# A fifth merged pair of weight rows in the second column half of w_out

## The chip, the cores and the metric

The kernel runs on one core of a Trainium2 chip. The metric is the device time of one execution in microseconds (us). Engines: TensorE (PE; PEld is its weight load), VectorE (DVE), ScalarE (ACT), GpSimd (POOL) and SyncE (SP), which here issues nearly all DMAs.

## The reference

One decoder layer on 256 tokens of width 2048, all in float32:

```
h = rms_norm(x);  proj = h @ w_in
o_sb = stick_breaking_attention(8 heads);  o_ds = indexed_sparse_attention(8 heads)
merged = sigmoid(g_sb) * (o_sb @ w_branch[:1024]) + sigmoid(g_ds) * (o_ds @ w_branch[1024:])
x = x + merged @ w_out                      # 2048 x 2048
h = rms_norm(x);  u = causal_depthwise_conv(h @ w_up)
x = x + (silu(gate) * val) @ w_down
```

The change is about `merged @ w_out`.

## The kernel before, in words

**Three matmuls for a product.** Every float32 operand is split into a high part and the rest (low). ACT makes the high part `hi` of a weight chunk, DVE subtracts it to make `lo`, and TensorE adds up three matmuls: left-high by right-high, left-low by right-high, left-high by right-low. One such group of three, 128 rows by 512 columns, is called a product here.

**Chunks and slots.** Weights come in chunks numbered through the program. There are four slots of `hi` and `lo` (`SLOTS`): chunk c uses slot c % 4, and ACT may write it once TensorE has used chunk c-4 (`w_used`). ACT and DVE run three chunks ahead (`AHEAD`): the loops over c in w_out (lines 1139 and 1825) start at C_OUT + 3 and hold, behind the split of each chunk, the other work of that stretch in a fixed order. All engines work in order.

**Plain and merged pairs.** w_out is done in two column halves (m = 0 and 1) of 1024 columns, each with eight pairs of 128-row tiles. A plain pair is two chunks of four products. A merged ("summed") pair is a Strassen-like form: four chunks, the first half as wide, with seven products together (`rows_summed`). It needs sums of weight blocks, here made far ahead by DVE in three additions (`weight_terms`), stored by a DMA in `out_sums` and loaded again like weights; and sums of the activation tiles `mT` with their high and low parts (`left_m`), made in batches (`sums_whole`, `sums_diff`, `sums_rest`, `left_hi_part`, `sums_lo`).

**Order in w_out.** `OUT_ORDER`: the first half has plain 4, merged 0 and 1, plain 5, merged 2 and 3, plain 6 and 7; the second has merged 0 and 1, plain 4, merged 2 and 3, plain 5, 6 and 7. Loads go through eight raw buffers (`OUT_SLOTS`) in the order of use, 48 loads in all; the raw buffers 0 to 3 serve the other stages too. SP issues a load when the low part of the chunk that held the buffer is done.

**Ends of the halves.** Behind the last merged pair of a half ACT copies four PSUM banks (`far_copy`), DVE adds them up in eight operations and adds them to y (`out_far`, lines 1795 to 1815). The other four banks are copied at the end of the first half (`near_copy`) and added to y (`out_near`); at the end of the second half DVE adds them straight from PSUM (line 1843). ACT takes squares of y for the norm (`square`), TensorE transposes y into `h2T`, with high and low parts by ACT and DVE, and w_up starts (`up_loads`, `up_body`).

**Where the weight sums come from.** Two of the eight sums are made in row block two of w_in (b = 1, `rows_turn` on SP, line 1631 on DVE), six in the gates stage (`spare_turn`).

Of the kernel before, what the change touches and what calls it, by code (L numbers as in the profile page):

```python
# [29 lines left out]
def hybrid_layer(nc, x, positions, attn_norm_g, w_in, q_norm_g, k_norm_g, w_branch, w_out,  # L30
# [9 lines left out]
    P = 128  # L40
# [41 lines left out]
    OUT_SUMMED = 4  # L82
    OUT_AT = [C_OUT + (2 * CPG + 2 * OUT_SUMMED) * m for m in range(3)]
# [4 lines left out]
    def block_steps(orders, chunk, raw, stored):  # L88

        table = []  # L90
        for b, order in orders.items():
            for kind, pair in order:
                made = pair if kind == "summed" else None
                table.append(Step(b, pair, made, chunk, raw, stored and made is not None))
                chunk += 2 if made is None else 4
                raw += 4 if table[-1].stored else 2
            assert chunk == BLOCK_END[b]
            assert sorted(p for _, p in order) == [*range(KT // 2)]
        return table

    def turns(*pairs):
# [5 lines left out]
                 [("summed", 0), ("summed", 1), ("plain", 4), ("summed", 2), ("summed", 3),  # L107
                  ("plain", 5), ("plain", 6), ("plain", 7)]]
# [6 lines left out]
    IN_ROWS, IN_SPARE = 2, 6  # L115
    OUT_SUMS = [(m, pair) for pair in range(OUT_SUMMED) for m in range(2)]
# [8 lines left out]
    OUT_SAVED = (C_UP - C_OUT) // SLOTS - OUT_EXTRA  # L125
    ROW_SLOT = [(q + SLOTS) % (SLOTS + 2) for q in range(ROW_RAWS)]
    ROW_SLOT += [q % OUT_SLOTS for q in range(OUT_RAWS)]
    assert OUT_RAWS % OUT_SLOTS == 0
# [18 lines left out]
    S_BATCHES = 2 * S_PAIRS // 2  # L147
# [23 lines left out]
    IN_BUFFER = (IN_ROWS + IN_GATES, IN_SPARE)  # L171
    IN_ALL = sum(IN_BUFFER)

    def spare_before(g):

        return 3 * IN_ROWS + 6 * g

    def gates_before(g):

        return 3 * IN_ROWS + 3 * g + 3 * (IN_SPARE if isinstance(g, int) and g >= IN_SPARE else g + 1)  # L180
# [47 lines left out]
    def summed(m, name):  # L228

        return len(ORDER[0]) * m + ORDER[m].index(name) + 1  # L230

# [11 lines left out]
    with ctx:  # L243
# [9 lines left out]
        def sem(name):  # L253
# [79 lines left out]
                  at("left_m", [OUT_SUMMED, 4, 2, P], 48 * KB, f32r)]  # L333
        whole_s = [at("whole_h", [2, 2, S], 74 * KB), at("whole_m", [2, 2, S], 64 * KB)]
        left_sraw = [at("left_hraw", [2, 4, P], 78 * KB), at("left_mraw", [2, 4, P], 68 * KB)]
        hsum13 = at("hsum13", [2 * GRP], 74 * KB)
# [47 lines left out]
        pre_spare = at("pre_spare", [4 * GRP], 96 * KB)  # L384
        sums = nc.dram_tensor("sums", (len(SUM_ROWS) * P, 4 * GRP), f32, kind="Internal").ap()
# [26 lines left out]
        def left_pairs(i):  # L412
            src, k, n = (hT, mT)[i // 2], 2 * (i % 2), left_count(i)
            return src[:, 2 * k:2 * (k + n), :].rearrange("p (b k) (q s) -> p b k q s", b=n, q=2)

        def left_count(i):
            return min(2, (S_PAIRS, OUT_SUMMED)[i // 2] - 2 * (i % 2))


# [168 lines left out]
        def _(sp):  # L588
# [48 lines left out]

            def rows_turn(j):
# [16 lines left out]
            def load_step(step, w, col):  # L655

                for k in range(4 if step.stored else 2):
# [9 lines left out]
                    elif stage(step) and slot < SLOTS + 2:  # L667
                        wait_alone(sp, sig_done, 8 * 4)
                    elif stage(step):
                        wait_alone(sp, left_done, S_BATCHES)  # L670
# [13 lines left out]
            def gates_turn(i):  # L684
# [4 lines left out]
                def before(j):  # L689
                    if j == 0:  # L690
                        wait_alone(sp, pre_stored[0], 16 * (IN_ROWS + i) + 1)
# [7 lines left out]
            def spare_turn(g, j):  # L699

                if j == 1 and 1 <= g <= IN_SPARE:
                    e = IN_ROWS + g - 1
# [3 lines left out]
                if j == 4 and g < IN_SPARE:  # L706
                    if g == 0:
                        wait_alone(sp, w_used, C_HEADS)
                    wait_alone(sp, pre_stored[1], 16 * g + 1)
                    out_terms(IN_ROWS + g, pre_spare, pre_landed[1])  # L710
# [14 lines left out]
            wait_alone(sp, pre_stored[1], 16 * IN_SPARE + 1)  # L725
# [34 lines left out]
            up_loads(0, {(1, 0): first_load})  # L760
# [49 lines left out]
        def _(act):  # L810
# [71 lines left out]
            def chunk_hi(c):  # L882
# [18 lines left out]
                act.activation(hi[s][:, 0:width], src[:, 0:width], ACT.Copy).then_inc(hi_done, 1)  # L901

            def left_hi_part(i):

                act.wait_ge(left4_raw, i + 1)
                at_, n = 2 * (i % 2), left_count(i)
                act.activation(left_s[i // 2][:, at_:at_ + n, :, 0, :],
                               left_sraw[i // 2][:, 0:n, :, :], ACT.Copy).then_inc(left_hi, 1)
# [74 lines left out]
            def block_out(c):  # L983

                for b, end in BLOCK_END.items():
# [14 lines left out]
                    if c == end + 2 and b == S_BLOCKS[0]:  # L1000
                        act.wait_ge(pre_stored[0], 16 * IN_ROWS + 1)
# [137 lines left out]
            for c in range(C_OUT + AHEAD, C_UP + AHEAD):  # L1139
                i = c - AHEAD - C_OUT  # L1140
                chunk_hi(c)
# [3 lines left out]
                if 20 <= c - OUT_AT[1] < 24:  # L1145
                    square(c - OUT_AT[1] - 20)
# [159 lines left out]
        def _(dve):  # L1306
# [106 lines left out]
            def chunk_lo(c):  # L1413
# [7 lines left out]
                else:  # L1421
# [5 lines left out]
                    .then_inc(lo_done, 1)  # L1427
# [34 lines left out]
            def sums_whole(i):  # L1462
# [6 lines left out]
                dve.tensor_tensor(whole_s[i // 2][:, 0:left_count(i), :, :], a[:, :, :, 0, :],  # L1469
                                  a[:, :, :, 1, :], ALU.add).then_inc(whole_done, 1)  # L1470

            def sums_diff(i):

                f, d = [x_[i // 2][:, 0:left_count(i)] for x_ in (whole_s, left_sraw)]
# [7 lines left out]
            def sums_rest(i):  # L1482

                f, d = [x_[i // 2][:, 0:left_count(i)] for x_ in (whole_s, left_sraw)]
# [7 lines left out]
            def sums_lo(i):  # L1492

                at_, n = 2 * (i % 2), left_count(i)
                left = left_s[i // 2]
                dve.wait_ge(left_hi, i + 1)
                dve.tensor_tensor(left[:, at_:at_ + n, :, 1, :], left_sraw[i // 2][:, 0:n, :, :],
                                  left[:, at_:at_ + n, :, 0, :].bitcast(f32), ALU.subtract)\
# [123 lines left out]
            for c in range(C_ROWS + AHEAD, C_HEADS + AHEAD):  # L1622
# [83 lines left out]
            def gates_body(h, spare):  # L1706
                for j in range(CPG):
# [25 lines left out]
                    if spare and j in (1, 2):  # L1733
                        for k in ((0,), (1, 2))[j - 1]:
                            weight_terms(pre_spare, pre_landed[1], 48 * h + 48, 3 * IN_ROWS + 6 * h, k)
                    if j in (5, 6, 7):
                        before = 3 * IN_ROWS + 3 * h + (3 * h + 3 if spare else 3 * IN_SPARE)
                        weight_terms(pre_gates, pre_landed[0], 48 * (IN_ROWS + h) + 48, before, j - 5)
                if not spare:
                    dve.wait_ge(pre_stored[1], 16 * IN_SPARE + 1)  # L1740
# [52 lines left out]
            def out_far(m, n):  # L1793
# [15 lines left out]
                if n == 2:  # L1809
                    dve.tensor_tensor(two[:, :], five[:, :], two[:, :], ALU.subtract)\  # L1810
# [507 lines left out]
        def _(pe):  # L2318
# [215 lines left out]
            def rows_plain(step, last):  # L2534
                for k in range(2):
# [11 lines left out]
                    i.then_inc(w_used, 1)  # L2547
# [5 lines left out]
            def rows_summed(step, end):  # L2553
                b, c, k = step.m, step.chunk, step.pair
                near, far = NEAR[b], FAR[b]
                left = left_s[stage(step)]
                s1, s2, s3, s4 = [(left[:, step.made, j, 0, :], left[:, step.made, j, 1, :])
                                  for j in range(4)]
# [244 lines left out]
```

## Time and profile before

| what | value |
|---|---|
| median of 3 runs | 1426.52 us (1426.42 to 1426.78) |
| profiled execution | 1426.08 us |
| its span | 1424.4 us |
| TensorE busy | 1418.9 us, 7583 matmuls |
| DVE busy | 1203.8 us |
| ACT busy | 902.8 us |
| DMA | 373.22 MB, mean 262 GB/s |

Busy means that an instruction of that engine was at work. Matmuls overlap and their ends are modelled, so the step from one product to the next is read from the starts. Times in the rows below are from the start of the span.

### The profile page before, as it was taken

The numbers are of one execution on the slowest core, as the hardware profiler recorded it, in microseconds if no ns is written. First come the engines' busy times: TensorE is split into PE (matmuls) and PEld (weight loads), VectorE is DVE, ScalarE is ACT, GpSimd is POOL, SyncE is SP. The second block draws the span as 40 slices with busy tenths as digits, with TensorE's granted clock in tenths as the row PEclk, the third lists the DMA queues.
The fourth block names the chain that finished last, engine by engine and source line by source line (L and its number), as shares of the span: only waits on it lengthen the run. The fifth ranks groups of instructions, "written<-read, shape, count | busy, mean of one in ns | idle before, by whom it ended". The sixth has DMA issues, their size and how long they took to land.

```text
span 1424.4 us, 23622 instructions
## 1 busy us (share of the span) xinstructions
PE 1418.9 (100%) x7583; PEld 1216.2 (85%) x7583; DVE 1203.8 (85%) x1591; ACT 902.8 (63%) x1302; POOL 329.6 (23%) x365
## 2 busy tenths in 40 slices
PE   9999999999999999999999999999999999999998
PEld 7888888888888888888888888888888888888887
DVE  6878998888878767887978888988889879898998
ACT  6546667566767766667665555555555556675775
POOL 2310000423232223560012222323223232100000
PEclk9999999999999999999999999999999999999999
DMA  8776665668999876569778888888888877698896
GB/s 256 243 249 183 208 197 185 194 183 293 312 337 329 285 232 209 186 239 336 258 237 279 275 292 289 279 281 279 290 289 276 280 221 233 232 318 315 312 339 250
DMA packets 151308, 373.22 MB, mean 262 GB/s; under 512 B 14048, under 2 KB 14336, under 8 KB 146768
## 3 DMA queue, kind: packets, MB, share of 16 engines
q1 hardware_dynamic: 150176, 369.93, 77.7%
q0 software_dynamic: 896, 2.42, 0.5%
q8 instruction: 29, 0.48, 0.1%
q14 instruction: 31, 0.25, 0.0%
q10 hardware_dynamic: 176, 0.14, 0.0%
HBM read 333.64 MB, written 38.80 MB: 261 GB/s over the span
## 4 chain that ended last, share of the span: by engine, by line
PE 99%; ACT 0%; DVE 0%; POOL 0%; issue 0%; DVEq 0%; POOLq 0%
PE bank L2320 98%; PE bank L2374 0%; PE bank L2393 0%; PE bank L2598 0%; ACT hT L837 0%; PE bank L2639 0%; DVE y L2008 0%; PE bank L2462 0%; POOL lo L2121 0%; ACT hi L820 0%; PE bank L2440 0%; DVE y L2053 0%; DVEq L243 0%; POOL ident L2101 0%; PE bank L2447 0%
## 5 line engine op out<-in xcount | busy, mean ns | idle before, releaser
L1311 DVE TENSOR_TENSOR lo<-raw,hi 128x1024 fp32r<-128x1024 f32 x338 | 436.6, 1297 | 140.4 <-ACT hi L820 138.6
L820 ACT ACTIVATE hi<-raw 128x1024 fp32r<-128x1024 f32 (+1 forms) x342 | 358.9, 1052 | 262.0 <-PE bank L2320 256.0
L2320 PE MATMUL bank<-h2T,hi 128*128 128x512 f32 x1408 | 483.3, 394 | 0.0
L2320 PE MATMUL bank<-h2T,lo 128*128 128x256 f32 x1408 | 376.8, 278 | 0.0
L2320 PEld LDWEIGHTS bank<-h2T,hi 128*128 128x128 f32 x1408 | 257.9, 188 | 53.5
L2320 PE MATMUL bank<-hT,hi 128*128 128x512 f32 (+1 forms) x784 | 272.9, 395 | 0.1
L2320 PEld LDWEIGHTS bank<-h2T,lo 128*128 128x128 f32 x1408 | 264.5, 188 | 7.8
L2320 PE MATMUL bank<-hT,lo 128*128 128x256 f32 (+1 forms) x784 | 212.6, 281 | 0.0
L1258 ACT ACTIVATE hi<-raw 128x1024 fp32r<-128x1024 f32 (+1 forms) x139 | 132.6, 974 | 64.2 <-PE bank L2320 63.2
L2320 PEld LDWEIGHTS bank<-hT,hi 128*128 128x128 f32 (+1 forms) x784 | 143.9, 187 | 29.8 <-POOL lo L2121 0.5
L1982 DVE TENSOR_TENSOR lo<-raw,hi 128x1024 fp32r<-128x1024 f32 (+1 forms) x139 | 152.2, 1124 | 16.1 <-ACT hi L1258 11.6
L2320 PE MATMUL bank<-hi,hT 128*128 128x512 f32 x520 | 161.7, 392 | 0.0
L2291 POOL TENSOR_TENSOR u<-u,rms_row 128x256 f32<-128x256 f32 x88 | 88.6, 1007 | 274.6 <-DVE u L1853 274.6
L2320 PEld LDWEIGHTS bank<-hT,lo 128*128 128x128 f32 (+1 forms) x784 | 147.0, 187 | 4.0
L2320 PE MATMUL bank<-hi,ffT 128*128 128x512 f32 x486 | 149.5, 389 | 0.0
L2320 PEld LDWEIGHTS bank<-hi,hT 128*128 128x128 f32 x520 | 96.6, 188 | 20.7 <-DVE lo L1425 0.5
L2320 PEld LDWEIGHTS bank<-hi,ffT 128*128 128x128 f32 x486 | 91.2, 188 | 18.9
L2320 PE MATMUL bank<-lo,hT 128*128 128x512 f32 x260 | 101.3, 390 | 0.0
L1863 DVE SCALAR_TENSOR_TENSOR conv<-u,params,conv 128x256 f32<-128x256 f32 x176 | 87.9, 500 | 12.3 <-DVE conv L1863 3.7
L2320 PE MATMUL bank<-lo,ffT 128*128 128x512 f32 x243 | 94.5, 389 | 0.0
L2305 POOL TENSOR_TENSOR conv<-conv,silu 128x256 f32<-128x256 f32 x44 | 60.4, 1373 | 116.3 <-DVE conv L1863 116.3
L2320 PE MATMUL bank<-oT,hi 128*128 128x512 f32 x256 | 86.9, 394 | 0.0
(293 smaller groups left out, 2021.8 us busy)
## 6 DMA issues: line engine op xcount, KB each, us to landing
raw<-in_w_up SPq DMA_DIRECT2D x176, 512.0 KB, 4.6
raw<-in_w_in SPq DMA_DIRECT2D x160, 512.0 KB, 4.6
raw<-in_w_down SPq DMA_DIRECT2D x61, 512.0 KB, 5.7
raw<-sums SPq DMA_DIRECT2D x54, 512.0 KB, 5.8
sums<-pre SPq DMA_DIRECT2D x19, 1024.0 KB, 6.3
raw<-in_w_branch SPq DMA_DIRECT2D x32, 512.0 KB, 4.2
pre<-in_w_down SPq DMA_DIRECT2D x19, 512.0 KB, 5.2
pre<-in_w_down SPq DMA_DIRECT2D x38, 256.0 KB, 5.6
```

Source lines behind the costliest of these rows:

```text
L820: act.activation(hi[s][:, 0:width], raw[s][:, 0:width], ACT.Copy)\
L1258: act.activation(hi[c % SLOTS][:, 0:width], src[:, 0:width], ACT.Copy)\
L1311: dve.tensor_tensor(lo[s][:, 0:width], raw[s][:, 0:width], hi[s][:, 0:width].bitcast(f32), ALU.subtract)\
L1863: dve.scalar_tensor_tensor(conv[b][ct % 2][:, :], u[b][ct][:, k:k + S], params[:, ds(column + e, 1)], conv[b][ct % 2][:, :], ALU.mult, ALU ...
L1982: dve.tensor_tensor(lo[s][:, 0:width], src[:, 0:width], hi[s][:, 0:width].bitcast(f32), ALU.subtract)\
L2291: pool.tensor_tensor(u[b][ct][:, 2:S + 2], u[b][ct][:, 2:S + 2], rms_row[:, :], ALU.mult).then_inc((gate_scaled, val_scaled)[b], 1)
L2305: pool.tensor_tensor(c, c, silu[ct][:, :], ALU.mult).then_inc(act_done, 1)
L2320: return pe.matmul(o, l, r, start=start, stop=stop, skip_group_check=True)
```

## The change

The second half of w_out merges pair 4 as well: its order is now merged 0 to 4 in a run, then plain 5, 6, 7. The ninth weight sum that this needs is made in row block two of w_in, in a buffer of its own (`pre_rows`); the sums of activation tiles for pair 4 are a fifth batch, made in the first half of w_out. There are now 50 loads in w_out. Since the half has two more chunks, two chunk numbers (22 and 23 from C_OUT, ahead of the first half's last pair) are skipped so that w_up starts at slot 0 again; `w_used`, `hi_done` and `lo_done` count over them with a step of three. The 50 loads end in the raw buffers 0 and 1, so SP waits for the last w_out low part ahead of the first w_up load and counts the buffers 2 and 3 on by hand. Some additions to y move to other chunks.

```
-    OUT_SUMMED = 4
-    OUT_AT = [C_OUT + (2 * CPG + 2 * OUT_SUMMED) * m for m in range(3)]
+    OUT_SUMMED = (4, 5)
+    OUT_SKIP = 2
+    OUT_AT = [C_OUT, C_OUT + 2 * CPG + 2 * OUT_SUMMED[0] + OUT_SKIP]
+    OUT_AT.append(OUT_AT[1] + 2 * CPG + 2 * OUT_SUMMED[1])
+    SKIPPED = range(OUT_AT[1] - 2 - OUT_SKIP, OUT_AT[1] - 2)
...
-                 [("summed", 0), ("summed", 1), ("plain", 4), ("summed", 2), ("summed", 3),
-                  ("plain", 5), ("plain", 6), ("plain", 7)]]
+                 [*[("summed", pair) for pair in range(5)], ("plain", 5), ("plain", 6),
+                  ("plain", 7)]]
...
+    LEFT_BATCHES = [(0, 0, 2), (0, 2, 2), (1, 0, 2), (1, 2, 2), (1, 4, 1)]
...
+    def passes(c):
+        return 1 + OUT_SKIP if c + 1 in SKIPPED else 1
...
             def rows_turn(j):
-                if j in (0, 10):
-                    wait_alone(sp, pre_stored[0], 1 + 16 * (j // 10))
-                    out_terms(j // 10, pre_gates, pre_landed[0])
-                if j in (8, 15):
-                    e = j // 15
-                    wait_alone(sp, pre_summed, 3 * e + 3)
-                    sp.dma_start(out_sums[e * P:(e + 1) * P, :], pre_gates[:, :])\
-                        .then_inc(pre_stored[0], 16)
+                if j == 0:
+                    wait_alone(sp, pre_stored[0], 1)
+                    out_terms(0, pre_gates, pre_landed[0])
+                if j == 6:
+                    wait_alone(sp, ss_done, 2 * TH)
+                    wait_alone(sp, pre_stored[1], 1)
+                    out_terms(1, pre_rows, pre_landed[1])
+                if j == 8:
+                    wait_alone(sp, pre_summed, 3)
+                    out_store(0, pre_gates, pre_stored[0])
+                if j == 10:
+                    wait_alone(sp, pre_stored[0], 17)
+                    out_terms(2, pre_gates, pre_landed[0])
+                if j == 12:
+                    wait_alone(sp, pre_summed, 6)
+                    out_store(1, pre_rows, pre_stored[1])
+                if j == 15:
+                    wait_alone(sp, pre_summed, 9)
+                    out_store(2, pre_gates, pre_stored[0])
...
+            def last_rows():
+                wait_alone(sp, lo_done, C_UP)
+                for slot in range(OUT_RAWS % OUT_SLOTS, SLOTS):
+                    sp.sem_inc(w_landed[slot], 16)
-            up_loads(0, {(1, 0): first_load})
+            up_loads(0, {(0, 0): last_rows, (1, 0): first_load})
...
+                    if c == end + 2 and b == NB - 1:
+                        act.wait_ge(pre_stored[1], 16 * IN_ROWS[1] + 1)
...
             for c in range(C_OUT + AHEAD, C_UP + AHEAD):          # ACT
                 i = c - AHEAD - C_OUT
-                chunk_hi(c)
+                if c not in SKIPPED:
+                    chunk_hi(c)
+                if i == 6:
+                    left_hi_part(4)
...
-                if 20 <= c - OUT_AT[1] < 24:
-                    square(c - OUT_AT[1] - 20)
+                if 22 <= c - OUT_AT[1] < 26:
+                    square(c - OUT_AT[1] - 22)
...
-                for e, terms_at in enumerate(((15, 16, 16), (24, 24, 24))):
-                    for k in range(3):
-                        if i == terms_at[k]:
-                            weight_terms(pre_gates, pre_landed[0], 48 * e + 48, 3 * e, k)
+                for k, at_ in enumerate((15, 16, 16)):
+                    if i == at_:
+                        weight_terms(pre_gates, pre_landed[0], 48, 0, k)
+                for k in range(3):
+                    if i == 20:
+                        weight_terms(pre_rows, pre_landed[1], 48, 3, k)
+                    if i == 24:
+                        weight_terms(pre_gates, pre_landed[0], 48 * 2, 6, k)
...
             for c in range(C_OUT + AHEAD, C_UP + AHEAD):          # DVE
                 i = c - AHEAD - C_OUT
-                chunk_lo(c)
+                if c not in SKIPPED:
+                    chunk_lo(c)
+                if i in (2, 3, 4):
+                    (sums_whole, sums_diff, sums_rest)[i - 2](4)
+                if i == 7:
+                    sums_lo(4)
...
-                for m, joins_at in enumerate(((7, 16, 17, 18), (7, 8, 9, 10))):
+                for m, joins_at in enumerate(((7, 14, 8, 17), (7, 8, 9, 10))):
...
-                if c - OUT_AT[1] in (18, 19):
-                    for o in ((0, 1), (2, 3))[c - OUT_AT[1] - 18]:
+                if c - OUT_AT[1] in (20, 21):
+                    for o in ((0, 1), (2, 3))[c - OUT_AT[1] - 20]:
                         out_near(o)
...
-                    i.then_inc(w_used, 1)
+                    i.then_inc(w_used, passes(c))
```

`joins_at` gives, for each half, how many chunks behind its last merged pair the four parts of `out_far` stand (parts 0 and 2 combine the copied banks, 1 and 3 add two of them each to y).

## Rows read from the trace of the kernel before

**Rows 1.** The page: span, busy time and share of each engine, TensorE's granted clock.
```profile
span 1424.4 us, 23622 instructions
...
PE 1418.9 (100%) x7583; PEld 1216.2 (85%) x7583; DVE 1203.8 (85%) x1591; ACT 902.8 (63%) x1302; POOL 329.6 (23%) x365
...
PEclk9999999999999999999999999999999999999999
```

**Rows 2.** Waits of TensorE, whole span: total us, times, longest us.
```profile
PE bank L2393 <- POOL ident L2101: 1.6, 1, 1.6
```

**Rows 3.** TensorE in order of time, w_out to w_up: start us, us.
```profile
706.56 0.62 PE L2320 MATMUL bank<-hi,mT 128*128 128x512 f32 x2
...
707.24 0.39 PE L2320 MATMUL bank<-h2T,hi 128*128 128x512 f32 x1
...
710.02 0.60 PE L2374 MATMUL bank<-ident,y 128*128 128x128 f32 x4
```

**Rows 4.** DVE in order of time, row block two; in brackets idle before it.
```profile
81.53 1.23 DVE L1311 TENSOR_TENSOR lo<-raw,hi 128x1024 fp32r<-128x1024 f32 x1 [2.65 <-ACT hi L820]
...
92.53 1.22 DVE L1611 TENSOR_TENSOR pre_gates<-pre_gates 128x1024 f32<-128x1024 f32 x1
...
95.26 1.22 DVE L1311 TENSOR_TENSOR lo<-raw,hi 128x1024 fp32r<-128x1024 f32 x1
```

**Rows 5.** DVE in order of time, first half of w_out.
```profile
632.65 2.37 DVE L1425 TENSOR_TENSOR lo<-raw67m,hi 128x512 fp32r<-128x512 f32 x2
634.94 2.55 DVE L1425 TENSOR_TENSOR lo<-raw,hi 128x1024 fp32r<-128x1024 f32 x2
638.02 2.50 DVE L1425 TENSOR_TENSOR lo<-raw,hi 128x1024 fp32r<-128x1024 f32 x2 [0.53 <-ACT hi L901]
```

**Rows 6.** ACT in order of time, change of halves; start of w_up.
```profile
657.61 0.63 ACT L901 ACTIVATE hi<-raw 128x512 fp32r<-128x512 f32 x1 [0.61 <-PE bank L2320]
660.33 1.06 ACT L901 ACTIVATE hi<-raw 128x1024 fp32r<-128x1024 f32 x1 [2.09 <-PE bank L2320]
...
664.01 1.07 ACT L977 ACTIVATE near_out<-bank 128x512 f32<-128x512 f32 x2
...
707.50 1.06 ACT L820 ACTIVATE hi<-raw 128x1024 fp32r<-128x1024 f32 x1 [1.66 <-PE bank L2320]
```

**Rows 7.** DVE in order of time, second half of w_out.
```profile
659.01 0.68 DVE L1425 TENSOR_TENSOR lo<-raw,hi 128x512 fp32r<-128x512 f32 x1
661.42 1.23 DVE L1425 TENSOR_TENSOR lo<-raw,hi 128x1024 fp32r<-128x1024 f32 x1 [1.72 <-ACT hi L901]
...
673.90 1.29 DVE L1791 TENSOR_TENSOR y<-y,far_out 128x512 f32<-128x512 f32 x2
675.11 1.22 DVE L1425 TENSOR_TENSOR lo<-raw,hi 128x1024 fp32r<-128x1024 f32 x1
```

**Rows 8.** DVE in order of time, end of w_out and start of w_up.
```profile
699.04 1.22 DVE L1425 TENSOR_TENSOR lo<-raw67m,hi 128x1024 fp32r<-128x1024 f32 x1
...
701.38 1.22 DVE L1311 TENSOR_TENSOR lo<-raw,hi 128x1024 fp32r<-128x1024 f32 x1
...
704.86 1.65 DVE L1336 SCALAR_TENSOR_TENSOR h2T<-bank,params,h2T 128x256 fp32r<-128x256 f32 x4
706.42 1.21 DVE L1311 TENSOR_TENSOR lo<-raw,hi 128x1024 fp32r<-128x1024 f32 x1
707.56 2.47 DVE L1791 TENSOR_TENSOR y<-y,bank 128x512 f32<-128x512 f32 x4
```

**Rows 9.** Loads: SP's issue; us to landing (from 693.6; all; from 665).
```profile
700.35 0.37 SPq L590 DMA_DIRECT2D raw<-in_w_up  x1
...
raw<-in_w_up SPq DMA_DIRECT2D x1, 512.0 KB, 3.8
...
raw<-in_w_up SPq DMA_DIRECT2D x176, 512.0 KB, 4.6
...
raw67m<-in_w_out SPq DMA_DIRECT2D x3, 512.0 KB, 8.4
```

More of the change, by code:

```diff
@@ L92, in block_steps @@
             for kind, pair in order:
+                chunk += OUT_SKIP if chunk in SKIPPED else 0
                 made = pair if kind == "summed" else None
@@ L114, in hybrid_layer @@
     OUT_SLOTS = SLOTS + 4
-    IN_ROWS, IN_SPARE = 2, 6
-    OUT_SUMS = [(m, pair) for pair in range(OUT_SUMMED) for m in range(2)]
+    IN_ROWS, IN_DVE, IN_SPARE = (2, 1), 3, 6
+    OUT_SUMS = [(m, pair) for pair in range(max(OUT_SUMMED)) for m in range(2)
+                if pair < OUT_SUMMED[m]]
     PART = {s.chunk + k: (s, k) for s in ROW_STEPS + OUT_STEPS
@@ L124, in hybrid_layer @@
     OUT_EXTRA = OUT_RAWS // OUT_SLOTS
-    OUT_SAVED = (C_UP - C_OUT) // SLOTS - OUT_EXTRA
+    OUT_SAVED = (C_UP - C_OUT) // SLOTS - OUT_EXTRA - 1
     ROW_SLOT = [(q + SLOTS) % (SLOTS + 2) for q in range(ROW_RAWS)]
     ROW_SLOT += [q % OUT_SLOTS for q in range(OUT_RAWS)]
-    assert OUT_RAWS % OUT_SLOTS == 0
+    assert OUT_RAWS == OUT_SLOTS * OUT_EXTRA + OUT_SKIP
     def first_turn(q):
@@ L170, in hybrid_layer @@
     IN_GATES = len(GATE_SUMS)
-    IN_BUFFER = (IN_ROWS + IN_GATES, IN_SPARE)
-    IN_ALL = sum(IN_BUFFER)
+    IN_BUFFER = (IN_ROWS[0] + IN_GATES, IN_ROWS[1] + IN_SPARE)
+    IN_ALL = IN_DVE + IN_SPARE + IN_GATES
     def spare_before(g):
-        return 3 * IN_ROWS + 6 * g
+        return 3 * IN_DVE + 6 * g
     def gates_before(g):
-        return 3 * IN_ROWS + 3 * g + 3 * (IN_SPARE if isinstance(g, int) and g >= IN_SPARE else g + 1)
+        return 3 * IN_DVE + 3 * g + 3 * (IN_SPARE if isinstance(g, int) and g >= IN_SPARE else g + 1)
     LAST_GROUP = STORED + 1
@@ L900, in chunk_hi @@
                 act.wait_ge(w_used, c - SLOTS + 1)
-                act.activation(hi[s][:, 0:width], src[:, 0:width], ACT.Copy).then_inc(hi_done, 1)
+                act.activation(hi[s][:, 0:width], src[:, 0:width], ACT.Copy)\
+                    .then_inc(hi_done, passes(c))
             def left_hi_part(i):
                 act.wait_ge(left4_raw, i + 1)
-                at_, n = 2 * (i % 2), left_count(i)
-                act.activation(left_s[i // 2][:, at_:at_ + n, :, 0, :],
-                               left_sraw[i // 2][:, 0:n, :, :], ACT.Copy).then_inc(left_hi, 1)
+                act.activation(share_made(i)[:, :, :, 0, :], share_diff(i)[:, :, :, :], ACT.Copy)\
+                    .then_inc(left_hi, 1)
             def first_block(i):
@@ L1482, in sums_rest @@
             def sums_rest(i):
-                f, d = [x_[i // 2][:, 0:left_count(i)] for x_ in (whole_s, left_sraw)]
+                f, d = share_whole(i), share_diff(i)
                 dve.wait_ge(left1_raw, i + 1)
@@ L1809, in out_far @@
                 if n == 2:
+                    dve.wait_ge(row_joined, before + 2)
                     dve.tensor_tensor(two[:, :], five[:, :], two[:, :], ALU.subtract)\
@@ L2555, in rows_summed @@
                 near, far = NEAR[b], FAR[b]
-                left = left_s[stage(step)]
-                s1, s2, s3, s4 = [(left[:, step.made, j, 0, :], left[:, step.made, j, 1, :])
-                                  for j in range(4)]
+                k_ = min(step.made, S_PAIRS)
+                left = left_five if k_ == S_PAIRS else left_s[stage(step)][:, k_:k_ + 1]
+                s1, s2, s3, s4 = [(left[:, 0, j, 0, :], left[:, 0, j, 1, :]) for j in range(4)]
                 pe.wait_ge(lo_done, c + 1)
```

61 lines of the change are left out of this document (38 added, 23 removed).

## The prediction

> **What bounds the kernel now.** I read the page first: TensorE is busy for the whole span at the full granted clock [rows 1]. The view of waits says the same: in 1424 us TensorE waited once, for 1.6 us, at the very start [rows 2]. So the kernel lasts as long as its matmuls follow each other. A change gains only by leaving matmuls out, and loses whenever something makes TensorE wait. The view in order of time gives the unit: one product (three matmuls of 512 columns) starts 0.68 us after the one before, 706.56 to 707.24 [rows 3]. The same view of ACT and DVE shows how narrowly TensorE is fed in w_out; all that follows is worked out there. Chunks are counted from C_OUT; "now" is the new numbering, in which 22 and 23 don't exist.
>
> **What it saves.** A plain pair has 8 products, a merged pair 7. One pair in w_out becomes merged: one product, **-0.68 us** [rows 3].
>
> **The price of feeding.** A chunk's high half takes ACT until 1.09 us after its start (660.33, DVE starts at 661.42), and the low half then takes DVE 1.23 us, or 1.15 us when another instruction stands behind it: 2.32 us from slot to usable weights [rows 6, 7]. A half-wide chunk takes 0.6 to 0.7 us on each. A merged pair thus costs DVE 0.60 + 3 x 1.15 = 4.05 us of TensorE's 7 x 0.68 = 4.76 us, a plain one 2.3 of 5.44 us. DVE has 0.7 us to spare in a merged pair, 3.1 us in a plain one. A slot is free 0.26 us after TensorE starts the following chunk: 707.24 against ACT's start at 707.50 [rows 3, 6].
>
> **Ninth sum in row block two.** DVE gets three terms, together 2.73 us (92.53 to 95.26). They stand behind score additions, after which DVE idles 2.65 us until 81.53 [rows 4]. The next low half slips by 0.1 us, and TensorE wants it some 5 us later. On SP there are three more loads and a store; the store waits for those terms, and the load behind it waits for the low half behind them anyway. ACT's new wait (end of row block 4) is for a store over 100 us old. Cost 0; if the cover were gone, 2.7 us at most.
>
> **Fifth batch of activation sums.** DVE gets, between chunks 5 and 10, a sum 512 wide (0.6 us), four operations 128 wide and a 512-wide low part; ACT one copy. In before, low halves 6 and 7 run from 632.65 to 635.02, the next two from 634.94, with some 0.6 to 0.8 us to spare for each, and the chain restarts at 638.02 after an idle 0.53 us [rows 5]. Ahead of chunk 8 stand 0.6 + 0.45 + 0.6 = 1.65 us of new work (estimates: the sum like a 512-wide low half's 0.68 [rows 7], each narrow one at 0.2 to 0.3, under half of that), less the spare: TensorE waits about **0.4 us**; bounds 0 and 1.6.
>
> **Two slots for four at the last plain pair.** Now chunk 24 has the slot of chunk 20 and chunk 25 that of 21. Count from TensorE's start of chunk 21, 657.35 (the row at 657.61 less 0.26). Chunk 24: slot free at 0.26, usable at 2.58, wanted at 2.72. Chunk 25: 2.98, 5.30, wanted at 5.44. The two far joins behind chunk 24 (1.2 us, as 673.90 to 675.11 [rows 7]) end at 3.7, ahead of chunk 25. Cost 0 with 0.14 us to spare, at worst 0.3 us.
>
> **Five merged pairs in a run.** In the same count TensorE wants chunks 26 to 31 at 8.16, 8.84, 10.20, 11.56, 12.92 and 13.60. Chunk 29 waits for the slot of chunk 25, at 8.42, and behind it ACT copies two banks (1.0 us, 664.01 [rows 6]), so the high half of 30 starts at 10.4, its low half at 11.06. Behind that stand two additions to y (1.21 us), which before stood at a plain pair (673.90 [rows 7]): low half 31 runs from 12.87 to 14.10, wanted at 13.60, **0.5 us** late. Two more additions behind chunk 33 end at 17.53; low half 35 ends at 19.36, wanted at 18.91, another **0.5 us**. From there DVE regains 0.7 us in each pair. Sum 1.0 us; bounds 0 (the wait absorbed by slack I did not see) and 2.4 (all four additions exposed).
>
> **The first weights of w_up.** This is the largest term. Fifty loads go through eight raw slots, so the last two lie in slots 0 and 1, and the new wait holds the first w_up load back until the low half of the last w_out chunk is done. Before, it was issued three chunks earlier, near 693.7. That low half ended at 699.04 + 1.22 = 700.26 (the load which waited for it was issued at 700.35), and TensorE began w_up at 707.24: a lead of 6.98 us [rows 3, 8, 9]. The end of block two keeps its pairs (plain 5, 6, 7), so I take this lead over. From the low half, as 0: issue 0.09, landing 3.8 later (an unloaded one; the median of all is 4.6 [rows 9]), high half, low half of chunk 52 starting at 0.09 + 3.8 + 0.05 + 1.09 = 5.03. DVE works in order, and behind that low half stand two additions, the next low half and the transposed tiles that TensorE wants before its first product. In before the low half of that first w_up chunk started at 701.38 and the second tile was ready at about 704.86 + 0.85 = 705.71, 4.33 us later [rows 8]. So w_up starts at 9.36 for 6.98: **2.4 us** of wait. Then the last additions to y: the second ends at 707.56 + 1.25, 7.43 us behind that low half, now at 12.46; TensorE is through its first chunk (2.78 us, 707.24 to 710.02) at 12.14 and waits **0.35 us** more [rows 3, 8]. The other three loads of the burst are wanted only later. With the median landing the two are 3.2 + 0.35. Bounds 0.9 (DVE's low halves at the very end running as early as the slots allow) and 4.5.
>
> **Sum.** -0.68 + 0 + 0.4 + 0 + 1.0 + 2.4 + 0.35 = +3.5 us. The profiled execution took 1426.08 us, so 1429.6 by its own time; the median shown is 0.44 us higher, and from there I predict **1430.0 us**.
>
> **Rivals.**
> *The w_up load is covered after all.* The point that decides is DVE's lead over TensorE at the last w_out low half: with 9.4 us instead of 7.0 nothing waits, which DVE would need to finish two chunks earlier than the additions let it. The trace speaks against it: from 699.04 on to the additions at 707.56 DVE shows no idle time [rows 8]. With the run's 1.0 and the 0.4 us paid, the time is 1426.5 - 0.7 + 1.4 = 1427.2; with neither, 1425.8. Neither is slower by what can be told.
> *Loads bound the run.* Five merged pairs want 3.5 loads of 512 KB in 4.76 us, with a place freed 6 to 8 us before its next weights are due. The slowest group of loads in this stretch has a median of 8.4 us to landing [rows 9], up to 2 us too late, of which 1.0 is slack. If that happened in three of the pairs, +3 us: 1433. Against it: the eight slots are full when the run begins.
> *The clock falls in the pause.* The rows show the full clock throughout and no pause of TensorE longer than 1.6 us, at which it stayed full [rows 1, 2]; a pause of 2.4 us or more is in no row. If the first w_up chunk ran at the lower level of 1.2 GHz, its 2.78 us would double: 1432.8. The Trainium skill ("TensorE: Matmul & The Clock Gate", Part 1: The HAM clock gate) says that the throttled clock is the default, that activity releases it, and that idling brings it back. By that rule the pause at the start of w_up is where it would show; the trace neither bears it out nor refutes it.
> *It doesn't do what it says.* Were the fifth merged pair no product fewer, 0.68 us would be missing from the gain: 1430.7, inside the forecast.
>
> **How the numbers follow.** Less than 0.2% (2.85 us) is no change here. Forecast with its terms as worked out, 1428.5 to 1432: 0.66. Load covered or nearly so, below 1428.5: 0.20. Loads bound the run: 0.09. Clock: 0.05. The line at 1429.4 cuts through the forecast: a little more than a fifth of it (0.15) lies below, where the run or the landing is kinder than my terms. So slower 0.51 + 0.09 + 0.05 = 0.65; the rest is "same", 0.31, but for 0.04 for faster, for which nothing in the rows offers the 2.85 us. The range takes the forecast, most of the covered case and part of the heavier two: 1427.0 to 1432.7.
>
> **What would show it.** Right: 7580 matmuls for 7583; a gap of TensorE of about 2.4 us ahead of its first matmul with h2T, ended by DVE's transposed tile, and a smaller one one chunk later, ended by y; the first w_up load issued just behind the last w_out low half; two waits of some 0.5 us for low halves in the second and third merged pair of the run; none in row block two. Wrong: no gap at the start of w_up, or ACT in the run waiting for landings instead of for TensorE's slots. The sum fails most easily at the landing time and at the lead of 7.0 us.

## The result: slower by half a per cent

The kernel after takes 1432.93 us, the median of six runs (1432.58 to 1434.73), against 1426.39 us for the kernel before on the same chip (six runs, 1425.98 to 1426.78): a ratio of 1.0049 [1.0036, 1.0062], +6.5 us. The direction was forecast; the forecast of 1430.0 us was 2.9 us too low, and the range ended 0.2 us short of the time. The profiled execution took 1432.95 us.

The page after, lines that answer to [rows 1]:
```profile
span 1431.2 us, 23647 instructions
...
PE 1420.8 (99%) x7580; PEld 1215.1 (85%) x7580; DVE 1211.7 (85%) x1602; ACT 905.0 (63%) x1305; POOL 327.7 (23%) x365
```
Three matmuls fewer: the product is saved. TensorE no longer fills the span, and the waits of TensorE over the whole span (total us, times, longest), which had one line in [rows 2], say on whom it waits:
```profile
PE bank L2380 <- DVE h2T L1385: 3.3, 1, 3.3
PE bank L2453 <- POOL ident L2161: 1.6, 1, 1.6
PE bank L2380 <- POOL lo L2181: 1.1, 2, 0.8
PE bank L2380 <- DVE lo L1474: 0.9, 3, 0.4
```
The ident line is the old one. The first line is the pause ahead of w_up, the last the waits in w_out. (POOL's lo belongs to the start of the kernel; its size differs from one profiled execution to the next, from nothing to 1.2 us.) The view counts an engine as waiting only once its modelled work has ended, so sizes below are read from the starts: a matmul of 512 columns normally starts 0.227 us behind the one before, and what a step has beyond that is lost. TensorE in order of time, after, first block of w_out, then the run:
```profile
635.20 0.39 PE L2380 MATMUL bank<-lo,mT 128*128 128x512 f32 x1
635.97 0.74 PE L2380 MATMUL bank<-hi,mT 128*128 128x512 f32 x2 [0.38 <-DVE lo L1474]
...
671.61 0.39 PE L2380 MATMUL bank<-lo,mT 128*128 128x512 f32 x1
672.33 0.74 PE L2380 MATMUL bank<-hi,mT 128*128 128x512 f32 x2 [0.33 <-DVE lo L1474]
...
677.00 0.39 PE L2380 MATMUL bank<-lo,mT 128*128 128x512 f32 x1
677.54 0.73 PE L2380 MATMUL bank<-hi,mT 128*128 128x512 f32 x2 [0.15 <-DVE lo L1474]
```
635.20 to 635.97 is 0.77 us, 0.54 us too long; three shorter ones behind it bring this place to 0.92 us. In the run 671.61 to 672.33 and 677.00 to 677.54 make 1.02 us with the step behind each.

The chain of waits, after, 703 to 717 us (start us, us, engine and what it did):
```profile
703.30 3.81 DMA raw<-in_w_up
...
707.13 1.07 ACT hi L864
...
708.23 1.23 DVE lo L1360
709.45 1.20 DVE y L1845 x2
710.65 1.14 DVE lo L1360
...
712.10 0.48 DVE h2T L1385
...
712.63 4.45 PE bank L2380 x16
```
The last w_out low half ends at 703.02, SP issues the load at 703.30, it lands at 707.11, and DVE passes the first low half, two additions, the second low half and the transposed tiles, in that order, until TensorE starts w_up at 712.63. Its previous matmul started at 708.90 (0.23 us of work): a pause of 3.50 us, none in [rows 3]. The windows of that stretch (us; busy time and instructions of PE, PEld, DVE, ACT, POOL; granted clock, with 1.00 for 2.4 GHz and 0.50 for 1.2; DMA share, at about 1 when the DMA engines are busy all the time; GB/s):
```profile
708.00:710.00 2.00, 1.29 (x6) 0.75 (x4) 1.77 (x3) 1.71 (x4) 0.00 (x0) 1.00 1.05 401
710.00:712.00 2.00, 0.00 (x0) 0.00 (x0) 2.00 (x4) 2.00 (x5) 0.00 (x0) 1.00 0.79 224
712.00:714.00 2.00, 1.37 (x4) 1.26 (x5) 2.00 (x5) 0.89 (x1) 0.00 (x0) 0.57 0.66 193
714.00:716.00 2.00, 2.00 (x9) 1.67 (x8) 2.00 (x4) 0.00 (x0) 0.00 (x0) 0.58 0.65 197
716.00:718.00 2.00, 2.00 (x15) 1.78 (x14) 2.00 (x4) 0.66 (x2) 0.00 (x0) 1.00 0.73 241
```
At the end of the pause the granted clock falls: it is 0.57 and 0.58, so mostly 1.2 GHz, from 712 until about 716. The first w_up chunk lasted from 712.63 to 716.92, 4.29 us instead of 2.78 [rows 3].

One more place lost time: in the run ACT waited for landings (waits of ACT, after, 660 to 700 us):
```profile
ACT hi L945 <- DMA raw45m<-in_w_out: 1.1, 2, 0.6
ACT hi L945 <- DMA raw<-in_w_out: 1.0, 1, 1.0
ACT hi L945 <- DMA raw<-out_sums: 0.8, 2, 0.6
ACT hi L945 <- DMA raw67m<-out_sums: 0.5, 1, 0.5
```
TensorE passed 0.45 us of it on, in steps at 687.22, 690.15, 691.41 and 691.75.

| place | forecast us | measured us |
|---|---|---|
| saved product | -0.68 | -0.68 (7580 matmuls) |
| ninth sum, row block two | 0 | 0 |
| fifth batch (635 to 638) | +0.4 | +0.92 |
| two slots for four | 0 | +0.08 |
| DVE in the run (671 to 678) | +1.0 | +1.02 |
| late loads in the run (687 to 692) | 0 | +0.45 |
| pause ahead of w_up | +2.4 | +3.50 |
| clock behind it | 0 | +1.51 |
| second wait, for y | +0.35 | 0 |
| sum | +3.5 | +6.8 |

As a control, from one fixed matmul ahead of w_out (the 3301st) to one in w_up (the 2000th from the end) the profiled execution after took 7.1 us longer than that of before; the difference of 0.3 us lies in steps too small to be listed. The same stretch is given for each experiment as "w_out, profiled". From the 101st matmul to the 501st, past the ninth sum, the two kernels agree within 0.01 us.

### The profile page after: what moved, and what is told of

Its sections match the earlier page's. It is cut to its first block, busy times and chain, and to the rows that moved or that the text cites. A ratio compares the mean times of both kernels' runs of the same rounds, so it can differ in the third digit from the quotient of the medians.

```text
span 1431.2 us, 23647 instructions
## 1 busy us (share of the span) xinstructions
PE 1420.8 (99%) x7580; PEld 1215.1 (85%) x7580; DVE 1211.7 (85%) x1602; ACT 905.0 (63%) x1305; POOL 327.7 (23%) x365
## 4 chain that ended last, share of the span: by engine, by line
PE 95%; DVE 2%; DMA 1%; ACT 1%; issue 0%; POOL 0%; DVEq 0%; SPq 0%; ACTq 0%; POOLq 0%
PE bank L2380 94%; DVE lo L1474 1%; DMA raw45m<-in_w_out 1%; DVE y L1845 1%; ACT hi L945 0%; DMA raw<-in_w_up 0%; PE bank L2658 0%; ACT hT L881 0%; PE bank L2434 0%; PE bank L2453 0%; PE bank L2699 0%; DVE lo L1360 0%; ACT hi L864 0%; DVE y L2068 0%; PE bank L2522 0%
```

## The experiments

Chunk numbers count from C_OUT, the two skipped numbers included. Differences are between medians, each against the kernel before on the same chip. A profiled execution that starts its first products late, as that of e5 did by 1.15 us against after's, is longer as a whole and not in its w_out stretch. "Late" steps are steps beyond 0.227 us, added up as above.

**e1: the first w_up load waits no longer.** After, but the 50 loads use the raw buffers so that the last four chunks leave buffers 0 to 3 to w_up as before.
```
-    ROW_SLOT += [q % OUT_SLOTS for q in range(OUT_RAWS)]
+    ROW_SLOT += [q % OUT_SLOTS if q < 24 else q - 20 if q < 26 else (q - 26) % OUT_SLOTS
+                 for q in range(OUT_RAWS)]
...
-            up_loads(0, {(0, 0): last_rows, (1, 0): first_load})
+            up_loads(0, {(1, 0): first_load})
```


> The changed kernel, but the w_out loads change raw buffers once (loads 24 and 25 take buffers 4 and 5 again), so that the last two loads lie in buffers 6 and 7, buffers 0 to 3 are free early, and the first w_up load waits for the low half three chunks before the last, as before the change. Theory A (the hold on the first w_up load costs a pause of 3.5 us and, behind it, 1.5 us at the lower clock): the gap ahead of the first matmul with h2T is gone, TensorE's clock stays full there, 1432.9 - 5.0 = 1427.9 us (1427.4 to 1428.5). Rival B (the run of five merged pairs leaves ACT and DVE so late, through its loads, that w_up starts late whatever its loads do): a gap of 1 to 3 us remains, 1429.5 to 1431.5 us.

1428.55 us (11 runs, 1427.95 to 1429.8), 1.0017 [1.0008, 1.0026], +2.4; w_out, profiled: +2.4. No gap ahead of w_up, and the clock at 1.00 there:
```profile
708.00:710.00 2.00, 2.00 (x11) 1.71 (x10) 2.00 (x5) 0.62 (x2) 0.00 (x0) 1.00 0.73 204
```
What is left is the rest of the table, with 0.93 us for late loads instead of 0.45: two buffers are used again after four and then six loads instead of eight. So the held-back load carried about 4 of the 6.5 us; of the 0.65 us by which theory A's 1427.9 was missed, 0.48 is the increase in late loads.

**e2: that wait alone.** Before, with nothing but the wait ahead of the first w_up load.
```
-            up_loads(0, {(1, 0): first_load})
+            up_loads(0, {(0, 0): lambda: wait_alone(sp, lo_done, C_UP), (1, 0): first_load})
```


> The kernel before, with one thing added: SP waits for the low half of the last w_out chunk ahead of the first w_up load. Nothing else of the change. Theory A: DVE's lead there is 6.98 us in this kernel, the path from that low half to TensorE's first product with h2T is 9.4 to 9.6 us, so a pause of 2.5 us; if the clock stays full through a pause of that length, 0.3 us more one chunk later and 1426.4 + 2.8 = 1429.2 us; if it falls as in the changed kernel, 1.5 us more instead, 1430.4 us. Rival B: without the run of five merged pairs the wait is covered, 1426.4 to 1427 us.

1430.14 us (9 runs, 1428.72 to 1430.98), 1.0027 [1.0017, 1.0037], +4.0; w_out, profiled: +3.9. Waits of TensorE, and windows behind them:
```profile
PE bank L2320 <- DVE h2T L1336: 2.1, 1, 2.1
```
```profile
708.00:710.00 2.00, 0.70 (x4) 0.65 (x5) 2.00 (x6) 1.59 (x2) 0.00 (x0) 0.97 0.80 243
710.00:712.00 2.00, 2.00 (x8) 1.62 (x6) 2.00 (x4) 0.00 (x0) 0.00 (x0) 0.50 0.70 238
712.00:714.00 2.00, 2.00 (x11) 1.73 (x10) 2.00 (x4) 0.00 (x0) 0.00 (x0) 0.68 0.77 215
```
From 706.81 to 709.30 no matmul starts: 2.27 us lost, close to the forecast's 2.4. The clock then falls to 0.50, and the first chunk takes 4.46 us (709.30 to 713.76) for 2.78, another 1.68 us; together 3.95, and the time near theory A's 1430.4 for a falling clock. One line thus costs 60% of the whole change, and over 40% of that price is the clock.

**e4: smaller loads in the run.** After, but in the second half only half the columns of the stored sums are loaded, and that part of the computation is left out.
```
-                        src = out_sums[row:row + P, (k - 2) * BLOCK:(k - 1) * BLOCK]
+                        width = GRP if step.m == NB + 1 else BLOCK
+                        src = out_sums[row:row + P, (k - 2) * BLOCK:(k - 2) * BLOCK + width]
```


> The changed kernel, but in the second half of w_out the loads of stored weight sums bring in only 512 of their 1024 columns (the other half of the buffer keeps what it had: that part of the computation is left out). Ten loads of 512 KB become 256 KB. Theory A (late loads cost 0.45 us directly and make DVE's lead at the end 0.86 us shorter): ACT no longer waits for landings between 681 and 692 us, the lead is 6.9 to 7.0 us, the pause ahead of w_up 2.6 us instead of 3.5; 1432.9 - 0.45 - 0.86 = 1431.6 us. Rival C (the lead is short because of the order of DVE's work, not because of loads): same time as the changed kernel within 0.3 us, 1432.6 to 1433.2 us.

1430.47 us (5 runs, 1430.14 to 1433.86), 1.0036 [1.0023, 1.0049], +4.3; w_out, profiled: +4.4. The steps of late loads are gone; those at 635 (0.88) and 671 to 678 (1.02) stay. The pause is 2.60 us (708.18 to 711.01): with the loads on time DVE's lead is the forecast one, so the late loads had cost the pause 0.9 us as well. The windows:
```profile
708.00:710.00 2.00, 0.57 (x3) 0.15 (x1) 2.00 (x3) 2.00 (x5) 0.00 (x0) 1.00 0.84 236
710.00:712.00 2.00, 0.99 (x5) 0.91 (x6) 2.00 (x6) 1.25 (x2) 0.00 (x0) 1.00 0.72 216
712.00:714.00 2.00, 2.00 (x12) 1.53 (x10) 2.00 (x4) 0.00 (x0) 0.00 (x0) 1.00 0.68 227
```
Here the clock stayed full, although the pause was longer than that of e2, which is why the time lies 1.1 us below theory A's; the wait for y behind it shows too, 0.2 us at 713.68.

**e5: the fifth batch later.** After, with the batch behind chunks 13 to 16 instead of 5 to 10.
```
-                if i in (2, 3, 4):
-                    (sums_whole, sums_diff, sums_rest)[i - 2](4)
-                if i == 7:
-                    sums_lo(4)
+                if i == 10:
+                    sums_whole(4)
+                if i == 11:
+                    sums_diff(4)
+                    sums_rest(4)
+                if i == 13:
+                    sums_lo(4)
```


> The changed kernel, but the fifth batch of activation sums stands eight to six chunks later in the first half of w_out, at the plain pair where DVE has idle time (sum at chunk 13, differences at 14, high part at 15, low part at 16 instead of 5, 6, 7, 9 and 10). Theory A (the batch made DVE late for chunks 7 and 9, 0.9 us of TensorE's time): the gaps at 635 and 637 us are gone, 1432.9 - 0.9 = 1432.0 us. Rival D (those gaps come from the loads, which ACT waited for at 632.5 and 633.8): the gaps stay, 1432.9 us.

1433.35 us (4 runs, 1432.55 to 1433.84), 1.0049 [1.0033, 1.0064], +7.2: no gain in time, against the expectation. In the trace the steps at 635 to 638 (0.92 us) are gone and 0.31 us at 651.28 has come; w_out, profiled: +6.3, 0.8 us less than after. Four runs can't show that: the profiled executions of these kernels reach their 101st matmul between 20.0 and 21.5 us, and e5's is the latest. The sum 512 wide, though, took half the time at its new place (DVE in order of time, after and then e5):
```profile
632.55 1.23 DVE L1518 TENSOR_TENSOR whole_five<-mT 128x512 f32<-128x512 f32 x1
```
```profile
643.44 0.69 DVE L1518 TENSOR_TENSOR whole_five<-mT 128x512 f32<-128x512 f32 x1
```

**e6: the additions apart.** e1, with the additions to y of the first half behind chunks 28 and 41 instead of 30 and 33.
```
-                for m, joins_at in enumerate(((7, 14, 8, 17), (7, 8, 9, 10))):
+                for m, joins_at in enumerate(((7, 12, 8, 25), (7, 8, 9, 10))):
```


> The kernel with early w_up loads (1428.5 us), and in it the two pairs of additions to y of the first half moved from behind chunks 30 and 33 to behind chunks 28 and 41. Theory A (1.0 us of TensorE's waits in the run come from these additions standing ahead of low halves 31 and 35): the gaps at 671 and 677 us are gone, 1428.5 - 1.0 = 1427.5 us. Rival F (the run costs this wherever the additions stand, since DVE or the loads bound it): the gaps come back further on in the run, 1428.2 to 1428.8 us.

1429.18 us (11 runs, 1428.75 to 1430.55), 1.0021 [1.0012, 1.003], +3.0: no gain over e1's +2.4; the 1427.5 us of theory A was missed, and the time lies above rival F's range too. The steps at 671 to 678 are gone, but between 674 and 689 others add up to 2.69 us, where ACT waits for DMAs. The windows of the run:
```profile
672.00:678.00 6.00, 5.55 (x24) 3.99 (x23) 4.11 (x5) 4.05 (x5) 1.07 (x2) 1.00 1.02 398
678.00:684.00 6.00, 5.88 (x26) 4.51 (x25) 5.07 (x5) 3.84 (x5) 0.54 (x1) 1.00 1.03 399
684.00:690.00 6.00, 5.52 (x22) 3.55 (x22) 5.29 (x8) 4.38 (x5) 0.54 (x1) 1.00 1.02 404
```
DMA share 1.02 at 398 to 404 GB/s, with DVE busy for 4.1 to 5.3 of 6 us: without DVE's work in front, TensorE waits for transfers. This run mixes two things, the moved additions and the early reuse of two buffers; e13 separates them.

**e7: the batch as well.** e6, with the fifth batch behind chunks 12 to 14.
```
+                if i == 9:
+                    sums_whole(4)
+                if i == 10:
+                    sums_diff(4)
+                    sums_rest(4)
+                if i == 11:
+                    sums_lo(4)
```


> The same, and the fifth batch of activation sums moved as well, to the plain pair of the first half (sum at chunk 12, differences at 13, high and low part at 14). Theory A: the gaps at 635 and 637 us (0.9 us) are gone and no new one comes at 651, 1427.5 - 0.9 = 1426.6 us. Rival D (TensorE's wait is only moved to another chunk): 1427.3 to 1427.6 us.

1427.6 us (11 runs, 1427.2 to 1429.32), 1.0011 [1.0002, 1.002], +1.4: 1.6 us under e6, of which the profiled stretch shows 0.9 (+3.2 to +2.3). No step is late in the first block, as theory A had it; 2.5 us stay in the run. The time itself lies in rival D's range, but only because both forecasts started from 1427.5 us, which e6 missed by 1.7.

**e8: less traffic in the run.** e7, with the loads of x for the second half, which POOL issues for the additions behind w_out, six to three chunks later (the first by six, the last by three).
```
-            for m, used in enumerate((C_OUT + 6, OUT_AT[1] + 6)):
+            for m, used in enumerate((C_OUT + 6, OUT_AT[1] + 12)):
...
-                        pool.wait_ge(w_used, used + (5 - 2 * m) * (2 * t + h))
+                        pool.wait_ge(w_used, used + (5 - 3 * m) * (2 * t + h))
```


> The same again, and the four loads of x for the second half (256 KB each) wait for six chunks more, so that fewer of them fall into the run of five merged pairs. Theory A (the late loads near 682 to 692 us, 0.9 us of TensorE's waits there, come from the DMA queues being full in the run): these waits shrink to 0.3 us or less, 1426.6 - 0.6 = 1426.0 us, and the kernel is as fast as before the change or a little faster. Rival G (a load is late because its buffer comes free late, whatever else is under way): same time within 0.2 us.

1426.19 us (11 runs, 1425.43 to 1427.18), 0.9999 [0.999, 1.0008], 1.4 us under e7. Of the steps beyond 680 us, 0.37 us is left. The largest step, 0.97 us at 673.77, belongs to a load that came 2.0 us late into one of the two buffers used again after six loads, so rival G had a part as well. (This profiled execution, 1427.18 us, was the longest of the 11.)

**e9: those two buffers used again at the end only.** e1, with the early reuse moved to the last two loads.
```
+    ROW_SLOT += [q % OUT_SLOTS if q < 48 else q - 44 for q in range(OUT_RAWS)]
```


> The changed kernel with early w_up loads once more, but the change of raw buffers stands at the very end: only the last two w_out loads take buffers 4 and 5 again, so in the run of five merged pairs each buffer is reused after eight loads as in the changed kernel (in the first such kernel two loads in the run followed after six). Theory A: no pause ahead of w_up, the rest as in the changed kernel, 1432.9 - 5.0 = 1427.9 us, 0.5 us under the first such kernel, whose two early reuses made loads late. Rival G (that reuse didn't matter): 1428.5 us again.

1428.03 us (11 runs, 1427.16 to 1431.36), 1.0017 [1.0008, 1.0026], +2.0; w_out, profiled: +2.0, so 5.1 us less than after, for the pause and the clock of the table (5.01). The other steps stand where after has them, 0.87, 1.02 and 0.52 us: -0.68 + 2.41 + 0.08 = +1.8.

**e12 and e13: is it the transfers?** Both are e9 with the additions of e6; e12 loads only half the columns of the sums in the second half, as e4, and leaves that part out; e13 loads all.

> The same, with the additions to y moved to behind chunks 28 and 41, and in the second half of w_out only 512 of 1024 columns of the stored weight sums loaded (the rest of the buffer keeps what it had: that part of the computation is left out). Theory H (the run has two bounds: with the additions moved away, the loads hold it up by as much; both must go): TensorE has no gaps in the run between 666 and 692 us, where the kernel with moved additions and full loads had 2.7 us; 1427.9 - 1.5 = 1426.4 us. Rival F (DVE's own work bounds the run wherever the additions stand): gaps of 1 us or more stay in the run, 1427.4 us or more.

> Early w_up loads with the buffers changed at the end only (1428.0 us), and in it the additions to y moved to behind chunks 28 and 41: full loads, x loads in the run, fifth batch where the change put it. It separates what the earlier kernel with moved additions mixed (1429.2 us): the loads of the run, and two buffers reused after six loads. Theory H (with the additions away, the loads of the run hold it up about as much): gaps of 0.7 us or more stay in the run, 1427.5 to 1428.0 us. Rival K (it was the early reuse of the two buffers): gaps of 0.4 us or less in the run, 1428.0 - 1.0 - 0.3 = 1426.7 to 1427.1 us.

e12: 1426.48 us (10 runs, 1426.3 to 1426.96), 1.0004 [0.9994, 1.0013], +0.4; in the run one place of 0.25 us is left. e13: 1427.29 us (11 runs, 1426.39 to 1428.66), 1.0007 [0.9998, 1.0016], +1.2; 0.87 us in the run, where e6, with the early reuse, had 2.69. The largest of e13's late steps, in order of time:
```profile
690.91 0.39 PE L2375 MATMUL bank<-lo,mT 128*128 128x512 f32 x1
691.47 0.73 PE L2375 MATMUL bank<-hi,mT 128*128 128x512 f32 x2 [0.17 <-DVE lo L1469]
```
So the additions' place is worth its 1.02 us if the loads are on time; of e6's loss most came from reusing two buffers early (1.8 of 2.69 us, and 1.8 between the medians of e6 and e13), and the amount of data accounts for most of the rest: 0.87 us of late steps at full size, 0.25 at half. e13's steps are those of theory H; its time fell between the two theories.

**e10: all of it.** e9 with the additions of e6, the batch of e7, and the loads of x behind chunks 41 to 44 (`OUT_AT[1] + 16`, one chunk apart).

> Early w_up loads (buffers changed at the end only), additions to y behind chunks 28 and 41, fifth batch at chunks 12 to 14, and the four x loads of the second half behind chunks 41 to 44, so that none falls into the run while weights are still on their way. Complete computation. Theory H: without x loads the run wants 385 GB/s, which the queues have delivered here (404 to 415 GB/s in full stretches), so its gaps shrink from 2.7 us to 0.5 us or less; 1426.2 - 0.68 + 0.5 = 1426.0 us, at best 1425.5. Rival F: gaps of 1.5 us stay, 1427 us.

1425.92 us (11 runs, 1425.39 to 1426.56), 0.9997 [0.9988, 1.0006] against 1426.03 for before (27 runs). The windows of the run, to be set beside e6's:
```profile
672.00:678.00 6.00, 6.00 (x28) 4.96 (x27) 5.51 (x6) 4.49 (x6) 0.00 (x0) 1.00 1.00 328
678.00:684.00 6.00, 6.00 (x28) 4.99 (x27) 5.52 (x7) 4.65 (x6) 0.00 (x0) 1.00 0.99 381
684.00:690.00 6.00, 6.00 (x27) 4.62 (x26) 6.00 (x7) 5.45 (x7) 2.14 (x4) 1.00 0.94 357
```
TensorE is busy throughout, with one place of 0.25 us at 685.17. Some 6.6 us better than after, it has the lowest median of all; but of the product's 0.68 us the trace leaves 0.32 (w_out, profiled: -0.32), and the timed runs don't tell it from before, nor from e8.

**e11: the run broken up.** e10 with plain 5 between merged 1 and 2, and the additions and squares placed for it.
```
-                 [*[("summed", pair) for pair in range(5)], ("plain", 5), ("plain", 6),
-                  ("plain", 7)]]
+                 [("summed", 0), ("summed", 1), ("plain", 5), ("summed", 2), ("summed", 3),
+                  ("summed", 4), ("plain", 6), ("plain", 7)]]
```


> The same kernel, but the five merged pairs of the second half are not in a run: merged 0 and 1, plain 5, merged 2, 3 and 4, plain 6 and 7; the first half's additions to y stand at plain 5, those of its near banks at plain 6. Complete computation. Theory H: a plain pair wants 193 GB/s and leaves DVE 3.1 us, so neither bound is met, no gap over 0.3 us in the second half; but the far banks of the second half are joined two chunks later, with up to 0.5 us at the start of w_up: 1425.5 to 1426.0 us. Rival J (the end with two plain pairs makes w_up late by more than 1 us): 1427 us or more, with the gap ahead of the first matmuls with h2T.

1431.38 us (5 runs, 1430.38 to 1431.86), 1.0038 [1.0024, 1.0052], +5.4, in rival J's range. The run has no late step, but the end pays (waits of TensorE, then ACT's longest in 660 to 700 us):
```profile
PE bank L2432 <- ACT far_out L1009: 2.5, 1, 2.5
...
PE bank L2432 <- DVE y L1840: 1.4, 1, 1.4
PE bank L2378 <- DVE h2T L1380: 1.0, 1, 1.0
```
```profile
ACT hi L940 <- DMA raw45m<-in_w_out: 5.0, 1, 5.0
```
The load of chunk 50 stands 5.0 us late in a buffer that the reuse at the tail frees late; ACT waits for it with the copies of the four banks behind. That one plain pair fewer at the end leaves this uncovered is argued: the additions and squares moved in the same run, and no run separates them.

## Why the prediction was right and wrong

The sum of the table is 3.3 us above the forecast's. Of that 1.5 us is the clock, put at nothing; 1.1 us the pause, 0.5 us the fifth batch and 0.45 us late loads; 0.35 us, the second wait, goes the other way.

**Right.** The saved product; the ninth sum at nothing; two slots for four at 0.08 us (0 to 0.3 forecast). The run's DVE term came where it was put, at the chunks behind the additions, 1.02 for 1.0 us, and e6, e12 and e13 show by moving the additions that they caused it. The held-back load is the largest term, as said: e1 takes it away and 4.2 us go (e9: 4.5), e2 adds it alone and 4.0 come, and the chain runs through the instructions that the forecast listed (landing 3.81 for 3.8, from the low half to TensorE 4.40 for 4.33).

**The pause was mis-sized, 3.5 us for 2.4.** Two numbers of that step failed. The lead of 6.98 us, "taken over" from [rows 3, 8], was 6.1 (703.02 to 709.13): ACT waited for late loads in the run, and DVE entered the end of w_out later. With smaller loads the pause is 2.60 us (e4), which gives 0.9 of the 1.1 us to the loads. And from low half to issue it took SP 0.28 us (703.02 to 703.30) for 0.09: in e2, with the wait but without the two semaphore increments ahead of the load, it was 0.16 (700.06 to 700.22), so some 0.12 us stands with the increments.

**The clock was put at 0; it cost 1.5 us.** This was a rival, at 0.05 and with 2.8 us. The trace agrees with the rule of the Trainium skill named there ("TensorE: Matmul & The Clock Gate", Part 1: The HAM clock gate) that idling brings the lower clock back, in that it fell at the pause of after, e2 and e5. The forecast's error was to treat "in no row" as improbable. What settles whether it falls stays open: it fell with pauses of 3.50 us (after), 3.49 (e5) and 2.27 us (e2) and not with 2.60 us (e4) or 2.61 (e11, at 699.57), so the length alone doesn't decide. Chance between executions of one kernel is possible but not shown: of e2's runs the two with a mean granted clock of 1.0 are the fastest (1428.72 and 1429.37 us; the others, at 0.998 or 0.999, took 1429.88 to 1430.98), and one of e4's, at 0.997, took 1433.86. But a run of after with a mean of 1.0 took 1432.63, and runs of before with 0.999 lost nothing, so this mean is too coarse to settle it. The second wait (forecast as 0.35 us, where its own numbers, 12.46 less 12.14, give 0.32) did not come, as the slow first chunk gave y time; with the full clock e4 has 0.2 us of it.

**The fifth batch was mis-sized, 0.92 us for 0.4.** The sum over 512 columns was taken like a low half of that width, 0.6 to 0.68 us [rows 7], and took 1.23. That is the step: with it the new work ahead of chunk 8 is about 2.2 us for 1.65 and, less the forecast's spare of 1.25, 0.95. The trace of before had a sign of it: the 512-wide low half in that very place, the first of the two in the first line of [rows 5], took as long.
```profile
632.65 1.23 DVE L1425 TENSOR_TENSOR lo<-raw67m,hi 128x512 fp32r<-128x512 f32 x1
```

**Late loads were put at 0; they cost 0.45 us in the run and 0.9 in the pause.** The rival "loads bound the run" (0.09) was true in part. The argument against it, that the buffers are full when the run begins, fails from the fourth merged pair on, where ACT first waits for a landing (at 682.22): over the run the transfers fall behind. The rows had the number (8.4 us to landing [rows 9]) but the forecast priced it as an all-or-nothing case.

## What to carry to other kernels

When a stage changes its number of loads, count where its ring of buffers ends: a first load of the next stage that has to wait for the last use of a buffer costs landing, split and all that the slower engine has queued, and behind the pause the lower clock can cost more: here 1.5 us with a pause of 3.50 us, 1.7 with one of 2.27, nothing with one of 2.60. A dense run that is tight on one engine should be checked on the next bound as well: with DVE's additions moved out, late transfers took their place, and only with less data in the run and even reuse of the buffers did the time come back to that of before. A saved product of 0.68 us can pay for neither the pause nor the clock, so the price of its feeding is worked out first.

## What the runs showed of the hardware

- **The clock after a pause.** It stayed full for most of the pause in after (1.00 until 712.2), was at 0.50 shortly before TensorE took up work (712.4 to 712.6, the first matmul at 712.63), and full again from 716. In e2 TensorE was at work first (709.30, 1.00 until 709.5), and the clock fell behind that (0.88 in 709.5 to 710, then 0.50). At the lower level matmuls of 512 columns start 0.427 us apart for 0.227.
- **A slow addition on DVE.** `whole_five` took 1.22 or 1.23 us in the seven traces with the batch at its first place (after, e1, e4, e6, e9, e12, e13), where POOL works on `br` (in after from 631.69 to 633.23, the addition from 632.55 to 633.78), and 0.68 or 0.69 us in the five with it later (e5, e7, e8, e10, e11), where POOL computes nothing. It goes with the place: the 512-wide low half which took 1.23 us there in before takes 0.68 in after, where it has slipped to 633.70. The Trainium skill ("GPSIMD Engine Reference", 1. Specifications) says that the two engines share their way into SBUF and that DVE's instructions with two SBUF inputs contend with POOL's; this one has two, and the twelve traces agree. So do other instructions of after: additions over 512 columns with both inputs in SBUF (`pre`) took 0.68 us where POOL was idle (19) and 1.12 to 1.24 where it computed (19), while `u<-bank,u`, with one input in PSUM, took 0.41 to 0.42 us either way (77 and 11). POOL's work was not varied by itself.
- **DMA busy throughout.** In the run the share of the DMA engines stands at 1.02 to 1.03 with 398 to 404 GB/s (672 to 690 us, e6), and a 512 KB load issued in 660 to 690 us landed a median of 7.9 to 9.2 us later, by kind, where one alone took 3.8 [rows 9].
